# Recurrent heads of a fused encoder layer: placing the small matrix products inside the weight chunks, and one activation table set per head

## What is computed

```python
f = lbf + (1.0 - lbf) * jax.nn.sigmoid(f_pre)
log_f = jnp.log(f)
k = 1.0 - f
...
b = jnp.cumsum(ll, axis=2)
o_inter = einsum('bhtd,bhdv->bhtv', qq * exp(b), S)
decay = exp(where(causal, b[t] - b[s], -inf))
A = einsum('bhtd,bhsd,bhtsd->bhts', qq, kk, decay)
o_intra = einsum('bhts,bhsv->bhtv', A, vv)
S_new = exp(b_last) * S + einsum('bhsd,bhsv->bhdv', kk * exp(b_last - b), vv)
...
o = o * rsqrt(mean(o * o) + EPS) * norm_g * silu(g)
```

## Time and profile before

| what | us |
|---|---|
| median of 3 runs | 2952.53 |
| lowest and highest run | 2952.22, 2954.99 |
| span of the profiled execution | 2950.9 |
| PE busy in it | 2872.7 |
| DVE busy | 1379.8 |
| ACT busy | 1141.4 |
| POOL busy | 625.0 |

### The profile page before, as it was taken

One profiled execution on the slowest core, in us unless ns is written; L12 is line 12 of the kernel. 1 busy time (PEld: TensorE's weight loads), 2 busy tenths in 40 slices (PEclk: granted clock), 3 DMA queues, 4 the chain that ended last, 5 costly groups with the idle time before them and its releaser, 6 DMA issues.

```text
span 2950.9 us, 34896 instructions
## 1 busy us (share of the span) xinstructions
PE 2872.7 (97%) x13685; PEld 2390.5 (81%) x13685; DVE 1379.8 (47%) x1618; ACT 1141.4 (39%) x1487; POOL 625.0 (21%) x257
## 2 busy tenths in 40 slices
PE   8999999999999999999999999999999999999998
PEld 7888878778877788878887788888888888888886
DVE  3354554510045400120427977777777775334333
ACT  6443544422244421232335544444444443223223
POOL 6433333234443344444332000000000000000000
PEclk9999999999999999999999999999999999999999
DMA  7322222223332233343233333333333336344432
GB/s 234 117 72 72 72 70 71 69 86 100 93 86 58 72 91 101 93 164 97 74 101 136 125 125 128 122 128 123 107 107 120 129 126 225 138 146 150 150 141 110
DMA packets 330543, 334.05 MB, mean 113 GB/s; under 512 B 26712, under 2 KB 234928, under 8 KB 327344
## 3 DMA queue, kind: packets, MB, share of 16 engines
q1 hardware_dynamic: 329808, 331.95, 34.5%
q10 hardware_dynamic: 608, 0.32, 0.0%
HBM read 311.25 MB, written 20.97 MB: 113 GB/s over the span
## 4 chain that ended last, share of the span: by engine, by line
PE 73%; DVE 4%; issue 1%; ACT 1%; DMA 1%; SPq 0%; ACTq 0%; DVEq 0%
PE psum L568 18%; PE psum L569 18%; PE psum L570 18%; PE psum L836 5%; PE psum L838 5%; PE psum L837 5%; PE psum L882 1%; DVE q_rot L1914 1%; PE psum L1069 1%; PE psum L787 1%; DMA f_raw<-in_w_down 1%; DVE f_lo L2082 0%; PE psum L768 0%; ACT swapped_t L1365 0%; DVE f_raw L2077 0%
## 5 line engine op out<-in xcount | busy, mean ns | idle before, releaser
L545 POOL TENSOR_TENSOR w_lo<-w_raw,w_hi 128x1024 fp32r<-128x1024 f32 x248 | 614.4, 2489 | 944.4 <-ACT w_hi L1146 943.2
L1492 ACT ACTIVATE f_hi<-f_raw 128x1024 fp32r<-128x1024 f32 x396 | 419.8, 1061 | 765.9 <-PE psum L570 502.5
L2082 DVE TENSOR_TENSOR f_lo<-f_raw,f_hi 128x1024 fp32r<-128x1024 f32 x392 | 479.6, 1224 | 472.9 <-ACT f_hi L1492 471.6
L568 PE MATMUL psum<-op_hi,w_lo 128*128 128x512 f32 x1216 | 488.3, 402 | 0.0
L569 PE MATMUL psum<-op_lo,w_hi 128*128 128x512 f32 x1216 | 478.7, 394 | 0.0
L570 PE MATMUL psum<-op_hi,w_hi 128*128 128x512 f32 x1216 | 478.1, 393 | 0.0
L1146 ACT ACTIVATE w_hi<-w_raw 128x1024 fp32r<-128x1024 f32 x248 | 257.9, 1056 | 238.5 <-PE psum L570 219.4
L568 PE MATMUL psum<-f_hi,pa_lo 128*128 128x512 f32 x704 | 274.2, 389 | 0.4 <-DVE f_lo L2082 0.4
L570 PE MATMUL psum<-f_hi,pa_hi 128*128 128x512 f32 x704 | 273.9, 389 | 0.0
L569 PE MATMUL psum<-f_lo,pa_hi 128*128 128x512 f32 x704 | 273.9, 389 | 0.0
L568 PEld LDWEIGHTS psum<-op_hi,w_lo 128*128 128x128 f32 x1216 | 231.9, 191 | 49.8 <-issue 2.6
(11 more groups left out here) (309 smaller groups left out, 4473.0 us busy)
## 6 DMA issues: line engine op xcount, KB each, us to landing
w_raw<-in_w_in SPq DMA_DIRECT2D x144, 512.0 KB, 3.8
f_raw<-in_w_gate SPq DMA_DIRECT2D x88, 512.0 KB, 4.6
f_raw<-in_w_up SPq DMA_DIRECT2D x88, 512.0 KB, 5.2
f_raw<-in_w_down SPq DMA_DIRECT2D x88, 512.0 KB, 4.7
pa_raw<-act_scratch SPq DMA_DIRECT2D x44, 512.0 KB, 4.0
w_raw<-in_w_out SPq DMA_DIRECT2D x32, 512.0 KB, 3.7
act_scratch<-c SPq DMA_DIRECT2D x22, 512.0 KB, 3.0
w_raw<-in_w_proj_a SPq DMA_DIRECT2D x16, 512.0 KB, 3.9
```

What stands on the lines that cost most here:

```text
L545: pool.tensor_tensor(w_lo[:, slot], w_raw[:, slot], w_hi[:, slot].bitcast(F32), ALU.subtract).then_inc(w_lo_ready, 1)
L568: pe.matmul(b[:, 0:n], wl, xh, start=start, stop=False)
L1492: act.activation(f_hi[i % FR][:, :], split_source(i)[:, :], ACT.Copy).then_inc(f_hi_ready, 1)
L2082: dve.tensor_tensor(f_lo[i % FR][:, :], split_source(i)[:, :], f_hi[i % FR][:, :].bitcast(F32), ALU.subtract).then_inc(f_lo_ready, 1)
```

## The change

On PE the second product of each pair of levels (1, 3, 5 and 7) moves from ahead of its chunk into the middle of it, and the key transposition moves with level 7. Where a step has no chunk at that place (step 8, c = 4 and 5) the order stays. In step 8 the gate chunks at c = 2 and 3 take the second product. On ACT each step that mixes asks, ahead of its first log, for the table set that holds log and exp. DVE, POOL and SP are not changed.

```diff
--- before.py
+++ after.py
@@ -665,6 +665,19 @@
                             last = pe.matmul(o, qk_lev[:, l % 2, f], right, start=True, stop=True)
                     last.then_inc(S("level_done"), 1)
 
+                def turn_kh():
+                    pe.wait_ge(S("khat_ready"), p + 1)
+                    before(pe, S("ln_mean"), 0, p, 1)
+                    for x in range(NB):
+                        f = slice(x * BLK, (x + 1) * BLK)
+                        last = pe.transpose(bank[5][:, f], kh_t[:, f], ident[:, :])
+                    last.then_inc(S("kh_turned"), 1)
+
+                def mid_chunk(c):
+                    level(2 * (c - 2) + 1)
+                    if c == 5:
+                        turn_kh()
+
                 for c in range(CK):
                     if c == 1 and tail:
                         pe.wait_ge(S("o_squared"), h - 1)
@@ -672,14 +685,10 @@
                         pe.matmul(bank[5], ones[:, :], osq_t[:, :], start=True, stop=True).then_inc(S("mean_done"), 1)
                     if mix and 2 <= c < 6:
                         level(2 * (c - 2))
-                        level(2 * (c - 2) + 1)
-                    if mix and c == 5:
-                        pe.wait_ge(S("khat_ready"), p + 1)
-                        before(pe, S("ln_mean"), 0, p, 1)
-                        for x in range(NB):
-                            f = slice(x * BLK, (x + 1) * BLK)
-                            last = pe.transpose(bank[5][:, f], kh_t[:, f], ident[:, :])
-                        last.then_inc(S("kh_turned"), 1)
+                        if not project and c not in gates:
+                            level(2 * (c - 2) + 1)
+                    if mix and c == 5 and not project:
+                        turn_kh()
                     if mix and c == 6:
                         pe.wait_ge(S("kh_nat_ready"), p + 1)
                         pe.wait_ge(S("v_nat_ready"), p + 1)
@@ -699,10 +708,11 @@
                             if x:
                                 last = pe.matmul(bank[6][:, f], state[:, x - 1, :], qe_t[:, f], start=False, stop=True)
                         last.then_inc(S("o_done"), 1)
+                    second = (lambda x=c: mid_chunk(x)) if mix and 2 <= c < 6 else None
                     if c in gates:
                         if c == 0:
                             pe.wait_ge(S("f_sig"), HEADS)
-                        gate_ahead(C_GA, gates[c])
+                        gate_ahead(C_GA, gates[c], middle=second)
                     if project and c == 6:
                         pe.wait_ge(S("vT_copied"), h + 1)
                         before(pe, S("v_nat_ready"), 0, h, 1)
@@ -720,7 +730,7 @@
                         if c == 6:
                             pe.wait_ge(S("vT_copied"), h + 1)
                         chunk(bank[c // 2 % 2], s0 + c, v, k, op_hi, op_lo, c % 2 * CK, KT,
-                              split_base=KT if first and c < 2 else None)
+                              split_base=KT if first and c < 2 else None, middle=second)
 
             pe.wait_ge(S("kv_copied"), XH + MT)
             head(0, 0, mix=False, tail=False, first=True)
@@ -1226,6 +1236,7 @@
                     if project:
                         split_hi(s0 + c + LEAD, v, k)
                     if c == 0 and mix:
+                        act.preload_act_table_set("natural_log_exp_and_others")
                         act.wait_ge(S("f_ready"), p + 1)
                         act.activation(log_f[:, :], f_t[:, :], ACT.Ln).then_inc(S("log_f"), 1)
                     if c == 0 and tail:
```

## The result

The changed kernel takes 2934.78 us, median of 4 runs (2934.45 to 2939.31), against 2953.41 of the kernel before beside it (4 runs, 2952.22 to 2954.99): ratio 0.9939, 95% interval 0.9925 to 0.9953.

What follows compares the result with a forecast made beforehand. PE, busy 97% of the span, was taken as the bound, with 24.5 us above its own pace. Terms -24.5, +3.9, +3.0 and 0 sum to -17.6 us, giving 2935 us, range 2927 to 2946.

Steps and rivals of the forecast that it cites:

- the main term: Heads 2 to 7: moving second products into mid-chunk removes PE's level 3 wait and the slow clock, -24.5 us.
- The wait at level 3 and the slow clock: Heads 2 to 7: PE's 2.0 us wait for the take of level 1 and the 1.2 GHz clock go, -24.5 us.
- The splits: Heads 1 to 8: 30 pairs taken apart each add a return to large matmuls at 0.13, +3.9 us (3.3 to 7.5).
- the lower bound of 0.11: Least cost in us of one return from small to large matmuls in mid-chunk, since every such return shows it.
- The new wait at level 6: PE waits at level 6 for DVE, held by POOL's splits: 0.5 us in six heads, +3.0 us (0 to 4.8).
- Heads 8 and 9: Last heads: level 3 wait and exp load go, but later levels and the angles' chain offset them, 0 (-4 to +1).
- The key transposition: Moved to mid-chunk on PE: keys ready in time, ACT's copy lands about 2 us before chunk 6, cost 0.
- The tables: ACT drops 24 table loads, 30.8 us, none PE time; spare beside the moved product, by itself half of each wait.
- No new wait: Rival: POOL's splits fall elsewhere; 2927 us if head 8's slow clock goes too, otherwise 2932; full gain (2927 to 2931) 0.15.
- The slow clock that stays: Rival: waits go but heads still drop to 1.2 GHz, 2946 us; chance 0.21, shared with new waits over 1 us.
- The wait that moves to level 6 at 2 us: Rival: PE waits 2 us at chunk 5 with the slow clock behind it, 2960 us; chance 0.06.
- The loads that don't go: Rival: the set is asked for again before each exp, ACT stays as it was, 2935 us too; no chance given.

Runs made afterwards that it cites:

- the run with half levels: Changed kernel with levels 1 and 7 issued in two halves in heads 1 to 7 (level 1 in head 8); 2939.56 us, one run.
- tables only: Kernel before, with the table set named once a head and PE's order as it was; 2936.29 us, ratio 0.9936.
- the mended kernel: Changed kernel with DVE's take of level 4 ahead of product 7 and levels 2 and 3 together in head 8; 2926.36 us, ratio 0.9905.
- the last experiment: Kernel before, with DVE taking level 1 right behind level 0 and the table set named once a head; 2932.26 us, ratio 0.9928.

## Why the prediction was right, and where its steps were not

The total was forecast at 2935 and the span's fall at 17.6; they came out at 2934.8 and 17.8. The mechanism of the main term held. That the sum is this close is luck: the splits cost 2.8 us less than forecast, heads 8 and 9 and the wait at level 6 cost 2.9 more, and the rest of the layer, which the change doesn't touch, happened to take the same time.

- **The wait at level 3 and the slow clock, -24.5.** Right. 327.93 is 347.91 - 24.5 + 0.9 (the splits of six periods at 0.15) + 3.7 (six waits at level 6 at 0.61), within 0.1. That the slow clock goes with the wait, which I only judged from head 1, is shown by three unlike remedies (PE's order, the tables, DVE's order), two of which leave PE's groups where they were: after waits of 0.2 to 1.0 us in heads 2 to 7 it never fell, after 2.0 us in the kernel before it fell five times out of six. Why not the sixth time is open.
- **The splits, +3.9.** Mis-sized. I read the return to large matmuls (5.57 against 5.44) and priced 30 of them at 0.13. In head 1 four splits cost 0.15 together, 0.04 each, and the run with half levels shows why: a group's entry gives back about what its return costs, and the lower bound of 0.11 looked at one side only. All of it was near 1.1 us, 2.8 too dear.
- **The new wait at level 6, +3.0 (0 to 4.8).** Right in place, in cause (splits of POOL back to back on DVE's operands) and in size: 0.36 us, six times, where I took 0.5. I missed two things: product 6 is what is held, both its ops, and a wait costs 0.25 beyond itself, so the term was 3.7. The Trainium skill (SBUF — State Buffer, SBUF: two separate sides) says that the engine which comes second at the shared ports is blocked until the first one's instruction is over. The trace agrees: 2.30 and 2.61 in place of 0.42 us under the two splits, and 0.41 for the second op when its split came later.
- **Heads 8 and 9, 0 (-4 to +1).** Wrong: +2.2. The step that failed is "with it level 5 and level 6 come 0.4 us or so later". Level 5 came about 0.7 later, but level 6 starts 20.2 us after head 8's level 0, before it was 18.5: 1.7 later. I followed product 5 and the take of level 3 down to level 5, and left out what stands behind DVE's last differences on ACT: the exp of level 7 and, behind it, the high part that POOL's split waits for. So the split came 1.8 us later and lay over product 6 (2.25 us in place of 0.63). The granted clock of the stretch fell to 0.85 from 0.88 as well. With tables only, where no level moves, it is 0.85 too and the stretch 0.9 longer, so how much of the 2.2 us is the moved level and how much the clock is open.
- **The key transposition, 0.** Right: no wait on it, none at chunk 6 in heads 1 to 7.
- **The tables, 0 beside the order.** Right: 24 loads, the op at 311.69 no longer waits, half of the wait left if they come alone. What the text left unsaid is that half a wait comes without the slow clock, so the part that I carried at nothing is worth 16 us alone. The Trainium skill (ScalarE: Activation LUTs, What ACT_TABLE_LOAD costs) gives about 2.66 us a switch, drain included. These rows don't show the drain: 30.8 us less ACT time for 24 loads is 1.28 each, with 0.1 us idle ahead of eight.
- **The rivals.** No new wait, 2927 to 2932: the wait came, 0.36 us in each of six heads, and the mended kernel, without it, takes 2926. The slow clock that stays: no. The wait that moves to level 6 at 2 us: it moved there, at 0.36; in head 8 it did reach 2.4. The loads that don't go: they went.

## What to carry to other kernels

Where one wait costs more than its length, because a slower clock follows it, several unlike remedies each earn nearly the whole and their sum earns no more: try the cheapest alone, here one line of DVE's order. Moving a product later is right only where nobody waits for it soon: look at who reuses its buffer, and at what stands in line behind that consumer on every engine, in each instance of the loop and in the last one most of all. Here the delay passed from DVE to ACT to POOL, and POOL's op then held DVE. For the price of a switch between kinds of matmul take a whole period with and without it, not the gap behind it alone.

## What the runs showed of the hardware

- Six waits of 2.01 us in otherwise equal heads: the clock fell to 1.2 GHz behind five of them (periods of 58.6 and 60.2, and 53.15 in head 7, which lacks a chunk) and not behind the first (57.06). Of 48 waits between 0.19 and 1.04 us in the same heads, six in each of the two profiles of the changed kernel and of six variants, none had it behind it. No wait between 1.04 and 2.01 us was tried in these heads.
- In head 8, where PE has less large work around the levels, the clock fell behind shorter waits. Behind 1.35 us at level 6 in the kernel before it was 0.76 from 556.03 to 558.40 and 0.50 from there to 567; behind 1.36 us with tables only it was 0.50 from 538.60 to 541.00. Behind 0.69 us in the mended kernel it was 1.00 from 531.80 to 537.00 and 0.61 in the 3.7 us after that.
- An op of DVE with a multiplication by a column (scalar_tensor_tensor) and two inputs in SBUF is held by POOL's split too: 2.79 us at 305.05 in the last experiment, with a split from 304.90 to 307.29, where the same op takes 0.75 at 312.54 in the kernel before. A take, with the new scores in PSUM, was not: 0.43 us at 534.18 in the changed kernel, with a split of POOL's running from 533.89.
- A wait of PE cost 0.22 to 0.25 us beyond its length, at full clock, in heads of three kernels (57.06 - 54.81 - 2.01; 55.57 - 54.96 - 0.36; 55.90 - 54.81 - 0.87, head 3 of tables only).
